# Gathered v rows by four slots of 32 tokens instead of one token's 128 slots, with scaled diagonals as stationary operand

## The chip, the cores and the metric

The kernel runs on one core of a Trainium2 chip. The metric is the device time of one execution in microseconds (us); the figure for the kernel before is the median of three runs. A profile of one further execution is read below. Engines are named as in the profile: PE is the matrix engine (TensorE), PEld its weight loads, DVE the vector engine, ACT the scalar engine, POOL the engine that issues the indirect transfers (GpSimd), SP the one that issues the weight blocks.

## The reference, cut to what matters

Two trunk layers are computed for 128 context tokens and for 256 latent tokens. Each layer has a mixer (four kinds of heads behind one input projection), and then the PEER stage, which is what the change is about:

```python
def peer(x, w_q, sub_keys, u_tab, v_tab):          # 8 heads, 16 of 16384 experts each
    q = (xt @ w_q).reshape(t, 8, 2, 128)
    s = einsum('thpc,hpkc->thpk', q, sub_keys)     # 2 x 128 sub-key scores a head
    s_top, i_top = top_k(s, 16)
    cand     = s_top[..0, :, None] + s_top[..1, None, :]        # 256 candidates
    cand_idx = i_top[..0, :, None] * 128 + i_top[..1, None, :]  # row = key1 * 128 + key2
    best, pos = top_k(cand, 16)
    idx  = take_along_axis(cand_idx, pos)          # (t, 128): 8 heads x 16 slots
    gate = softmax(best)
    act  = gelu(einsum('ted,td->te', u_tab[idx], x))
    return einsum('te,ted->td', gate * act, v_tab[idx])
```

For every token 128 rows of 1024 float32 (4 KB) are fetched from table u and 128 from table v. Row number is key1 x 128 + key2, so two rows with the same second key lie a multiple of 512 KB apart. A token's 16 rows of one head come from a 16 x 16 grid of keys and often share one.

## The kernel before, in words

There are six tiles of 128 tokens, q = 0 to 5: q0 is the context in layer 0, q1 and q2 the latent tokens in layer 0, q3 the context in layer 1, q4 and q5 the latent tokens in layer 1. They form four units: unit 0 is q0, unit 1 is q1 with q2, unit 2 is q3, unit 3 is q4 with q5. Each unit has a mixer; the u and v work of the unit before is interleaved with it by a fixed table (`schedule`, `mix_points`): at given points of its own stream every engine runs the next `item_u` or `item_v` (`gap`). The u and v work of unit 3 has no mixer beside it and makes up the last 720 us.

Gathers. POOL issues one indirect transfer per step s (line 501), 128 rows of 4 KB, one row into each partition of ring slot s % 8. So the ring holds eight transfers, and a slot is refilled only when its reader has raised `rows_used` for it. In a u transfer, partition p holds the row of token p at slot s. In a v transfer before the change, partition p holds slot p of one token, `token(s)` = (s % 4) * 32 + s // 4; its indices are column `token(s)` of `idxT`, which is the transposed table of indices.

v sums. `item_v` on PE works in half steps of four transfers, one for each group of 32 tokens. Each group has its own 32 columns of the PE array and its own 32 partitions of the accumulator `pv`. For each transfer there are two matmuls (512 of the 1024 columns each) with a stationary operand of 128 x 32 from `wcol`. A float32 matmul shows as two records in the profile, so a transfer has four, and all of them together 3072. Before the change the stationary operand is zero but for column m, which holds the token's 128 weights. The zeros are written once (line 1362). ACT writes the eight columns of the next step in one ACTIVATE (`fill_wcol`, line 1310), four buffers deep: the fill for step i+2 waits until PE has used step i-2. PE releases the four slots of a half step during its second matmuls, that is after the fourth transfer has landed.

Start of a tile's v work (`item_gelu` on three engines): ACT runs Gelu on the dot products, DVE multiplies by the gates (line 1844), PE transposes the 128 x 128 result (line 952), ACT copies it to `wT` and fills `wcol` for the steps 0 and 1, and PE's first half step waits for the first fill (line 966). The index table is transposed on PE at the end of a tile's top-k (line 1002) and DVE copies it to `idxT` (line 1808) before it goes on with the gates.

Lines that the prediction speaks of: L501 (POOL, gathers), L524 and L527 (the helpers through which every matmul and every transpose goes), L966 and L971 (PE's waits for the fill and for the rows), L1017 (the helper of every ACTIVATE), L1310 (fill), L1362 (memset), L1808 and L1844 (DVE), L1838 (DVE's dot product of a u transfer).

## Time and profile before

| | |
|---|---|
| median of three runs | 3166.04 us (3154.32 to 3171.97) |
| span of the profiled execution | 3176.3 us |
| PE busy / PEld busy | 63% / 37% |
| DVE busy | 56% |
| POOL busy | 47% (1536 gathers) |
| ACT busy | 12% (814 instructions) |
| gathers' share of the 16 DMA engines | 68.0%, 805.4 MB |
| last 720 us (q4 and q5, u then v) | DMA busy 9 tenths or more in nearly every slice |

The profiled execution has no separate time beside its span; the span is 10.3 us over the median of the runs and 4.3 us over the slowest. In the page, the line of 40 slices gives the busy share of each engine in tenths, 79.4 us a slice. A group's row gives the line, the engine, the operation, what is written and read, the shape and the count, then busy time (overlaps counted once) and the mean duration of one. Where instructions overlap, busy time over count is less than that mean, and it is busy time over count that says how fast they follow each other. A row of the timeline gives the start, the duration and in brackets how long the engine sat idle before, and what ended that.

### The profile page before, as it was taken

The numbers are of one execution on the slowest core, as the hardware profiler recorded it, in microseconds if no ns is written. First come the engines' busy times: TensorE is split into PE (matmuls) and PEld (weight loads), VectorE is DVE, ScalarE is ACT, GpSimd is POOL, SyncE is SP. The second block draws the span as 40 slices with busy tenths as digits, with TensorE's granted clock in tenths as the row PEclk, the third lists the DMA queues.
The fourth block names the chain that finished last, engine by engine and source line by source line (L and its number), as shares of the span: only waits on it lengthen the run. The fifth ranks groups of instructions, "written<-read, shape, count | busy, mean of one in ns | idle before, by whom it ended". The sixth has DMA issues, their size and how long they took to land.

```text
span 3176.3 us, 27801 instructions
## 1 busy us (share of the span) xinstructions
PE 2008.3 (63%) x10194; PEld 1164.2 (37%) x10194; DVE 1763.4 (56%) x3957; ACT 378.2 (12%) x814; POOL 1480.1 (47%) x1540
## 2 busy tenths in 40 slices
PE   5979386668887414438878776677897000067777
PEld 3858275564732413402341165563751000011111
DVE  1622699872286899950070079984176999910000
ACT  1322121112201100000110021112210000000000
POOL 0000144324156565666526634324137777766664
PEclk7979697869998756679989978777999555589999
DMA  6557487547589999999969978656579999999998
GB/s 242 204 197 294 154 338 295 185 150 278 179 288 365 412 385 341 361 379 371 371 229 368 362 279 325 200 171 225 179 252 330 401 410 409 406 364 365 357 352 309
DMA packets 249063, 959.26 MB, mean 302 GB/s; under 512 B 32352, under 2 KB 33504, under 8 KB 231136
## 3 DMA queue, kind: packets, MB, share of 16 engines
q0 software_dynamic: 221184, 805.40, 68.0%
q1 hardware_dynamic: 19584, 142.62, 12.1%
q10 hardware_dynamic: 8160, 9.46, 0.9%
q8 instruction: 82, 1.34, 0.2%
q14 instruction: 53, 0.43, 0.0%
HBM read 955.01 MB, written 2.36 MB: 301 GB/s over the span
## 4 chain that ended last, share of the span: by engine, by line
DVE 26%; DMA 26%; PE 25%; POOL 13%; issue 7%; ACT 2%; ACTq 1%; POOLq 0%; DVEq 0%
PE pb L524 17%; DMA sb_ring<-in_peer_v,sb_idxT 16%; DVE sb_ring L1838 13%; POOL sb_ring L501 13%; DMA sb_ring<-in_peer_u,sb_idxu 8%; PE pv L524 7%; DVE sb_big L1402 1%; PE pb L527 1%; DVE sb_big L1531 1%; DVE sb_big L1550 1%; DVE sb_dec L1492 1%; ACT sb_hT L1017 1%; ACT sb_big L1017 1%; DMA sb_dec<-in_x_prompt 1%; DVE sb_big L1548 1%
## 5 line engine op out<-in xcount | busy, mean ns | idle before, releaser
L501 POOL DMA_INDIRECT sb_ring<-in_peer_u,sb_idxu x768 | 727.9, 948 | 965.4 <-DVE sb_dots L1838 460.9
L501 POOL DMA_INDIRECT sb_ring<-in_peer_v,sb_idxT x768 | 752.0, 979 | 710.0 <-PE pv L524 477.1
L524 PE MATMUL pv<-sb_ring,sb_wcol 128*32 128x512 f32 x3072 | 816.2, 638 | 212.1 <-DMA sb_ring<-in_peer_v,sb_idxT 203.8
L1838 DVE CUSTOM_DVE_ANT_0 sb_ring<-sb_ring,pv 128x1024 f32<-128x1024 f32 x768 | 904.2, 1217 | 27.6 <-DMA sb_ring<-in_peer_u,sb_idxu 14.5
L524 PEld LDWEIGHTS pv<-sb_ring,sb_wcol 128*32 128x32 f32 x3072 | 145.5, 112 | 848.5 <-DMA sb_ring<-in_peer_v,sb_idxT 655.5
L524 PE MATMUL pb<-sb_hT,sb_wring 128*128 128x256 f32 (+1 forms) x1888 | 366.9, 357 | 32.4 <-DMA sb_wring<-in_w_in_blocks 12.7
L524 PEld LDWEIGHTS pb<-sb_hT,sb_wring 128*128 128x128 f32 x1888 | 323.5, 206 | 78.5 <-issue 16.3
L524 PE MATMUL pb<-sb_big 128*128 128x128 f32 (+2 forms) x1888 | 266.5, 315 | 112.9 <-DVE sb_big L1531 82.1
L524 PEld LDWEIGHTS pb<-sb_big 128*128 128x128 f32 (+1 forms) x1888 | 259.7, 225 | 125.1 <-DVE sb_big L1531 87.0
L527 PE MATMUL pb<-sb_cst,sb_dots 128*128 128x128 f32 x6 | 2.7, 451 | 402.1 <-DVE sb_dots L1844 402.1
L1851 DVE COPY sb_accv<-pv 128x1024 f32<-128x1024 f32 x6 | 7.3, 1224 | 392.6 <-PE pv L524 392.5
L524 PE MATMUL pb<-sb_big,sb_cst 128*128 128x256 f32 (+2 forms) x272 | 101.5, 533 | 107.4 <-DVE sb_big L1470 42.2
L1017 ACT ACTIVATE sb_big<-pb 128x512 f32<-128x512 f32 (+3 forms) x184 | 84.9, 467 | 549.8 <-PE pb L524 421.3
L527 PEld LDWEIGHTS pb<-sb_cst,sb_dots 128*128 128x128 f32 x6 | 1.1, 175 | 403.6 <-DVE sb_dots L1844 403.6
L1739 DVE MAX8 sb_xe<-sb_dec 128x8 f32<-128x128 f32 x128 | 28.1, 281 | 171.5 <-ACT sb_cv L1017 94.4
L524 PEld LDWEIGHTS pb<-sb_big,sb_cst 128*128 128x128 f32 x272 | 57.9, 247 | 140.3 <-DVE sb_big L1470 43.9
L1808 DVE CAST sb_idxT<-pb 128x128 uint32<-128x128 f32 x6 | 1.8, 292 | 183.6 <-PE pb L527 183.4
L1732 DVE SCALAR_TENSOR_TENSOR sb_xT<-pb,sb_modT,sb_xT 128x128 f32<-128x128 f32 (+1 forms) x32 | 13.4, 417 | 156.5 <-PE pb L524 156.5
L524 PE MATMUL pb<-sb_wring,sb_hT 128*128 128x256 f32 x336 | 82.8, 408 | 18.6 <-ACT sb_big L1017 14.1
L1017 ACT ACTIVATE sb_wcol<-sb_wT 128x8 f32<-128x8 f32 x96 | 18.3, 212 | 522.4 <-PE pv L524 522.3
L524 PEld LDWEIGHTS pb<-sb_wring,sb_hT 128*128 128x128 f32 x336 | 69.0, 208 | 30.1 <-issue 14.9
L1017 ACT ACT_TABLE_LOAD x57 | 73.1, 1283 | 9.4 <-issue 5.1
(220 smaller groups left out, 1868.0 us busy)
## 6 DMA issues: line engine op xcount, KB each, us to landing
sb_wring<-in_w_in_blocks SPq DMA_DIRECT2D x32, 1024.0 KB, 8.0
sb_ring<-in_w_mod_blocks SPq DMA_DIRECT2D x30, 1024.0 KB, 5.2
sb_wring<-in_w_q_blocks SPq DMA_DIRECT2D x27, 1024.0 KB, 4.9
sb_wring<-in_w_mod_blocks SPq DMA_DIRECT2D x18, 1024.0 KB, 5.0
sb_wring<-in_w_out_blocks SPq DMA_DIRECT2D x13, 1024.0 KB, 7.9
sb_ring<-in_peer_u,sb_idxu POOLq DMA_INDIRECT x768, 7.3
sb_ring<-in_peer_v,sb_idxT POOLq DMA_INDIRECT x768, 6.1
sb_ring<-in_w_in_blocks SPq DMA_DIRECT2D x8, 1024.0 KB, 5.3
```

The costliest lines, as they stand in the source:

```text
L501: pool.indirect_dma_start(ring[:, j, :], None, a["tab_" + kind][l_of(q)], bass.IndirectOffsetOnAxis(ap=of, axis=0)).then_inc(rows_in[j], 16)
L524: return nc.tensor.matmul(out, lhsT, rhs, start=start, stop=stop)
L527: return nc.tensor.transpose(out, in_, ident[0:in_.shape[0], 0:in_.shape[0]])
L1017: return nc.scalar.activation(out, in_, f, **kw)
L1402: last = stt(y, cin[:, k % 2, n:n + NC], convT[:, k, n:n + 1], y, ALU.mult, ALU.add)
L1492: last = stt(dec[:, d, m * 4 + h, :], pb[:, 2 * d + m, h * P:h * P + P], gct[:, i, c:c + 1], con("negm", d, P), ALU.subtract, ALU.add)
L1531: return tt(dst, big_at(512 * d, 4, P), bc1(lvl[:, d, lv, :], 4), ALU.mult)
L1548: tt(x, x, pb[:, 2 + d, :], ALU.add).then_inc(*tick("x_ready", (u, i, d, lv)))
L1550: tt(xt, xt, pb[:, 4 + d, :], ALU.add).then_inc(*tick("xt_ready", (u, i, d, lv)))
L1732: stt(x, pb[:, 4 + j % 2, 0:NC], modT[:, l, 16 + j, g:g + 1], x, ALU.mult, ALU.add) \
L1739: last = dve.max(vals(r)[:, lo:lo + 8], rows(r))
L1838: dve.tensor_tensor_reduce(out=ring[:, j, :], in0=ring[:, j, :], in1=pv[:, :, :].rearrange("p a b -> p (a b)"), scale=1.0, scalar=0.0, op0 ...
```

## The change: what it does, and the diff

A v transfer now takes slots b, 32+b, 64+b and 96+b of the 32 tokens of one group g: partition j*32+a holds the row of token g*32+a at slot j*32+b. For this the tables of indices and of weights are not transposed as a whole but turned in blocks of 32 x 32 (`turn_blocks`): 16 matmuls with 32 columns of the identity as stationary operand, in place of one transpose. Column `turned(s)` = (s % 4) * 32 + s // 4 of the turned tables then serves transfer s. A partition's row now goes to the token of its own lane, so the stationary operand is a diagonal of 32 x 32 in each of the four blocks, scaled by the weight of the partition: ACT makes it from a constant `lane` (128 x 32 of zeros and ones) with the scale read from `wT`, one ACTIVATE for a transfer, eight for a step. As a whole block is written each time, the zeros around the column and their memset go. The number, size and order of gathers, the ring, the matmuls of the v sum and all waits stay as they are.

```diff
-WCOL_WIDTH = STEP * LANES + LANES
+WCOL_WIDTH = STEP * LANES
...
+    parts["lane"] = i[:, None] % LANES == np.arange(LANES)[None, :]
...
-        def token(s):
+        def turned(s):
             return s % GROUPS * LANES + s // GROUPS
...
-                    of = idxu[:, t, s:s + 1] if kind == "u" else idxT[:, t, token(s):token(s) + 1]
+                    of = idxu[:, t, s:s + 1] if kind == "u" else idxT[:, t, turned(s):turned(s) + 1]
...
+            def turn_blocks(bank, src):
+                for gr in range(GROUPS):
+                    for j in range(GROUPS):
+                        last = mm(pb[j * LANES:j * LANES + LANES, bank, gr * LANES:gr * LANES + LANES],
+                                  ident[:, gr * LANES:gr * LANES + LANES], src[:, j * LANES:j * LANES + LANES])
+                return last
...
             def item_gelu(q, t):
                 pe.wait_ge(*done("w_ready", q))
                 take([2], ("wT_copied", q))
-                tr(pb[:, 2, 0:P], dots[:, t, :]).then_inc(*tick("wT_full", q))
+                turn_blocks(2, dots[:, t, :]).then_inc(*tick("wT_full", q))
...
-                                o = j * LANES + LANES - 1 - m
+                                o = j * LANES
                                 last = mm(pv[gr * LANES:gr * LANES + LANES, k, :], wcol[:, i % WCOLS, o:o + LANES],
                                           ring[:, j, k * 512:k * 512 + 512], start=m == 0, stop=m == LANES - 1)
...
-                tr(pb[:, 4, 0:P], posf[:, 0, :]).then_inc(*tick("idxT_full", q))
+                turn_blocks(4, posf[:, 0, :]).then_inc(*tick("idxT_full", q))
...
             def fill_wcol(nv, c):
-                dst = wcol[:, c % WCOLS, LANES - 1:LANES - 1 + STEP * LANES].rearrange("p (m g x) -> p m g x", g=GROUPS, x=LANES)
-                src = wT[:, :].rearrange("p (g m) -> p m g", g=GROUPS)
-                fn(dst[:, :, :, 0], src[:, 2 * c:2 * c + 2, :]).then_inc(wcol_ready, 1)
+                for j in range(STEP):
+                    w = turned(STEP * c + j)
+                    last = fn(wcol[:, c % WCOLS, j * LANES:j * LANES + LANES], con("lane"), ACT.Identity, scale=wT[:, w:w + 1])
+                last.then_inc(wcol_ready, 1)
...
-                dve.memset(wcol[:, :, :], 0.0)
```

ACT's order around the start of tile q0's v work in the mixer of unit 1, before (`sb_dots` is Gelu, `sb_wcol` the fills, the rest is the mixer's; shapes are partitions x elements):

```order
194 L1017 ACTIVATE sb_dots<-sb_dots 128x128
195 L1017 ACTIVATE sb_wT<-pb 128x128
196 L1017 ACTIVATE sb_wcol<-sb_wT 128x8 x3
197 L1017 ACTIVATE sb_big<-pb 128x256 x4
198 L1017 ACTIVATE sb_dec<-pb 128x256 x2
199 L1017 ACTIVATE sb_wcol<-sb_wT 128x8
200 L1017 ACT_TABLE_LOAD
201 L1017 ACTIVATE sb_sm<-sb_sm,sb_epsc 128x2x6
```

The same place of the changed kernel:

```order
194 L1027 ACTIVATE sb_dots<-sb_dots 128x128
195 L1027 ACTIVATE sb_wT<-pb 128x128
196 L1027 ACTIVATE sb_wcol<-sb_cst,sb_wT 128x32 x24
197 L1027 ACTIVATE sb_big<-pb 128x256 x4
198 L1027 ACTIVATE sb_dec<-pb 128x256 x2
199 L1027 ACTIVATE sb_wcol<-sb_cst,sb_wT 128x32 x8
200 L1027 ACT_TABLE_LOAD
201 L1027 ACTIVATE sb_sm<-sb_sm,sb_epsc 128x2x6
```

Nothing changes places; every fill has eight instructions in place of one, and no table load is added (57 in both).

PE's order at the end of unit 3's mixer and in the last 720 us, before (`sb_big` is the index table of q4 and of q5, `sb_dots` the weights, `pv<-sb_ring,sb_wcol` the v sum, one row per instruction of the program, not per record):

```order
443 L524 MATMUL pv<-sb_ring,sb_wcol 32x512 x64
444 L527 MATMUL pb<-sb_cst,sb_big 128x128
445 L524 MATMUL pv<-sb_ring,sb_wcol 32x512 x72
446 L527 MATMUL pb<-sb_cst,sb_big 128x128
447 L524 MATMUL pv<-sb_ring,sb_wcol 32x512 x8
448 L527 MATMUL pb<-sb_cst,sb_accv 128x128 x8
449 L527 MATMUL pb<-sb_cst,sb_dots 128x128
450 L524 MATMUL pv<-sb_ring,sb_wcol 32x512 x256
```

The same place of the changed kernel:

```order
443 L526 MATMUL pv<-sb_ring,sb_wcol 32x512 x64
444 L526 MATMUL pb<-sb_big,sb_cst 32x32 x16
445 L526 MATMUL pv<-sb_ring,sb_wcol 32x512 x72
446 L526 MATMUL pb<-sb_big,sb_cst 32x32 x16
447 L526 MATMUL pv<-sb_ring,sb_wcol 32x512 x8
448 L529 MATMUL pb<-sb_cst,sb_accv 128x128 x8
449 L526 MATMUL pb<-sb_dots,sb_cst 32x32 x16
450 L526 MATMUL pv<-sb_ring,sb_wcol 32x512 x256
```

Here too nothing changes places: twelve transposes in the program (two for each of the six tiles) become 16 small matmuls each.

## Rows read from the trace of the kernel before

**Rows 1.** The page, busy tenths in 40 slices of 79.4 us.
```profile
DVE  1622699872286899950070079984176999910000
DMA  6557487547589999999969978656579999999998
```

**Rows 2.** Busy time in stretches: us, PE, PEld, DVE, ACT, POOL, clock, DMA share, GB/s.
```profile
2680.00:2780.00 100.00, 0.00 (x0) 0.00 (x0) 95.22 (x155) 0.00 (x0) 72.54 (x78) 0.50 1.02 406
2800.00:2960.00 160.00, 126.16 (x448) 21.99 (x440) 0.00 (x0) 2.81 (x13) 104.68 (x112) 1.00 0.98 366
2839.40:2843.40 4.00, 3.52 (x15) 0.79 (x16) 0.00 (x0) 0.00 (x0) 1.77 (x3) 1.00 1.02 412
2845.60:2849.00 3.40, 2.77 (x12) 0.52 (x12) 0.00 (x0) 0.22 (x1) 2.53 (x3) 1.00 0.84 271
2849.60:2855.60 6.00, 5.14 (x18) 0.79 (x16) 0.00 (x0) 0.00 (x0) 3.72 (x4) 1.00 1.04 416
```

**Rows 3.** Chain of waits, 2838 to 2864 us: start, us, what.
```profile
2839.16 6.57 DMA sb_ring<-in_peer_v,sb_idxT
2845.77 1.08 PE pv L524 x6
...
2850.83 6.32 DMA sb_ring<-in_peer_v,sb_idxT
```

**Rows 4.** Groups that touch sb_wcol and other ACT and PE groups, shapes apart.
```profile
L1017 ACT ACTIVATE sb_wcol<-sb_wT 128x8 f32<-128x8 f32 x96 | 18.3, 212 | 522.4 <-PE pv L524 522.3
L1017 ACT ACTIVATE sb_hT<-sb_hT,sb_modT,sb_modA 128x256 f32<-128x256 f32 x32 | 16.2, 587 | 16.4 <-DVE sb_hT L1383 16.4
L1017 ACT ACTIVATE sb_cv<-sb_big,sb_lay 128x128 f32<-128x128 f32 x20 | 8.0, 400 | 93.9 <-DVE sb_big L1402 93.7
L524 PE MATMUL pv<-sb_ring,sb_cpad 128*32 128x256 f32 x480 | 39.0, 451 | 7.1 <-ACT sb_modrow L1017 6.3 <-ACT sb_solW L1017 0.8
L524 PEld LDWEIGHTS pv<-sb_ring,sb_cpad 128*32 128x32 f32 x480 | 14.8, 122 | 17.5 <-issue 10.8 <-ACT sb_solW L1017 1.2
L527 PE MATMUL pb<-sb_cst,sb_dots 128*128 128x128 f32 x6 | 2.7, 451 | 402.1 <-DVE sb_dots L1844 402.1
```

**Rows 5.** Timeline of ACT, a run of one mixer group.
```profile
818.16 4.04 ACT L1017 ACTIVATE sb_hT<-sb_hT,sb_modT,sb_modA 128x256 f32<-128x256 f32 x8 [4.04 <-DVE sb_hT L1383]
```

**Rows 6.** Timeline, start of the v work of q4.
```profile
2792.38 4.59 PE L524 MATMUL pv<-sb_ring,sb_wcol 128*32 128x512 f32 x18 [0.85 <-ACT sb_wcol L1017]
2794.66 0.20 PEld L524 LDWEIGHTS pv<-sb_ring,sb_wcol 128*32 128x32 f32 x7 [1.08 <-DMA sb_ring<-in_peer_v,sb_idxT]
2796.38 0.93 POOL L501 DMA_INDIRECT sb_ring<-in_peer_v,sb_idxT  x1 [3.10 <-PE pv L524]
```

**Rows 7.** Chain of waits, start of the v work of q5.
```profile
2977.96 0.34 PE pb L527
...
2978.63 0.43 ACT sb_wcol L1017 x3
...
2979.10 2.94 PE pv L524 x13
```

**Rows 8.** Timeline, ACT and DVE in the mixer of unit 1.
```profile
724.02 0.21 ACT L1017 ACTIVATE sb_wcol<-sb_wT 128x8 f32<-128x8 f32 x1
725.98 0.30 ACT L1017 ACTIVATE sb_sm<-sb_sm,sb_epsc 128x12 f32<-128x12 f32 x1 [0.44 <-DVE sb_sm L1663]
813.92 0.21 ACT L1017 ACTIVATE sb_wcol<-sb_wT 128x8 f32<-128x8 f32 x1
```

**Rows 9.** Timeline, DVE at the end of unit 3's mixer; then DVE's memsets at the start.
```profile
2451.87 0.29 DVE L1808 CAST sb_idxT<-pb 128x128 uint32<-128x128 f32 x1 [23.73 <-PE pb L527]
...
2.16 1.02 DVE L1362 MEMSET sb_wcol<- 128x1152 f32 x1 [0.19 <-issue]
```

**Rows 10.** Timeline, ACT at the program's start.
```profile
6.24 0.22 ACT L1017 ACTIVATE sb_cpad<-sb_cT 128x16 f32<-128x16 f32 x1 [1.69 <-DMA sb_cT<-in_cT]
```

## The prediction

> **What bounds the kernel now.** I read the line of slices first [rows 1]. In the last nine slices, the 720 us without a mixer, the DMA line is at 8 or 9 tenths throughout. In the first four of them DVE is at 9 (the u work of q4 and q5), in the last four at 0 (the v work, whose sums PE makes). So the gathers bound this part, and the two kinds run unlike: 406 GB/s in a stretch of u, 366 GB/s in a stretch of v [rows 2]. The reader should see that the DMA share is 1.02 in the first and still 0.98 in the second. Whether the v rows are dear to fetch or come too late is the question on which this change turns.
>
> Short stretches of the v part answer it [rows 2]. From 2839.4 to 2843.4 and from 2849.6 to 2855.6 the engines move 412 and 416 GB/s, as fast as in any u stretch. Between them, from 2845.6 to 2849.0, they move 271 GB/s at a share of 0.84. The chain of waits shows why [rows 3]: the last transfer of a half step is issued at 2839.16 and lands 6.57 us later, PE then needs 1.08 us until slots are free, POOL refills four slots, and the last of these goes out at 2850.83, 4.0 us later. From issue to issue that is 11.67 us for eight transfers. At 412 GB/s eight transfers of 0.524 MB would take 10.2 us, and at the stretch's mean of 366 GB/s a round is 11.5 us. The v loop is bound by the round trip through a ring of eight that is released in fours, not by what a row costs. About 1.3 us in each round are dry.
>
> **The gathers after the change.** Count, bytes, slots, waits and the order of release stay. If a fed queue already moves 412 GB/s with the old pattern, another pattern has nothing to speed up there. I take 0 for 768 transfers. Bounds: at best most of the dry time goes, 1.1 us a round, if it is in truth the slow rows that cause it (rival A); at worst the new pattern slows rows. The u transfers, 128 tokens at one slot, mix tokens as the new ones do and reach 406 GB/s, so I put the worst at 0 too.
>
> The pattern itself does change: rows that share their second key lie a multiple of 512 KB apart, and the 16 rows of a head of one token share keys more often than rows of 32 different tokens. The Trainium skill (DMA: Bandwidth & Descriptors, section on latency and other measured facts) has a table on HBM row pitch: copies with a pitch of 512 KiB between partitions reach 207 GB/s, 2 MiB 164, 4 MiB 103, against 214 with a padded pitch. By its first figure the old pattern would lose some 3%, and by the last, for the few pairs that lie 4 MiB apart, more; rival A is what this rule makes of the time. The 412 GB/s of the fed stretches speak against it.
>
> **The fills on ACT.** One ACTIVATE for a step becomes eight with 32 elements and a scale from memory. Nearest rows: 12 elements with one operand column take 0.30 us [rows 8], 128 elements with one 400 ns [rows 4], so 32 take about 320. Neighbours overlap: 32 ACTIVATEs with two operand columns are busy 16.2 us, 506 ns each, where one lasts 587 ns [rows 4], and three old fills take 0.43 us together at 0.21 each, 0.11 us apart [rows 7]. With 80 to 100 ns of overlap I take them 0.22 us apart: 0.32 + 7 x 0.22 = 1.85 us for a fill against 0.21, that is 1.6 us more. Bounds: without any overlap 8 x 0.32 = 2.6, so 2.4 more; at the old spacing 8 x 0.11 = 0.9, so 0.7 more. Over 96 fills ACT gets 155 us of work more. It is 12% busy, so this counts only where somebody waits:
> - Steady v work: the fill of step i+2 is made when step i-2 is used, two rounds of 11 us ahead. Cost 0; the 522 us that ACT waits for PE before fills [rows 4] hide it.
> - In the mixers ACT makes the fill in its own order and whatever follows waits. After the fill at 813.92 the next ACTIVATE starts at 818.16, 4 us later [rows 5, 8], and so it is for most of the 64 fills there: more than 1.6 us of slack. The exception is 724.02, which a table load and the tiny `sb_sm` follow; that one waited 0.44 us only for DVE [rows 8], and DVE waits for it. There are three such places (one each in units 1, 2 and 3, the one in unit 2 with two fills together): 1.2 + 3.2 + 1.2 = 5.6 us at most. I take 2, since behind them PE has v steps to do.
> - At the start of each tile's v work PE waits for the first fill: 1.6 us more each.
>
> **The turned blocks on PE.** A transpose of 128 x 128 lasts 0.45 us [rows 4]. In its place come 16 matmuls, 32 records. The trace has no matmul with 32 x 32 outputs. The nearest has a 32-column stationary operand, in the four column groups in turn, with 256 columns: 480 records in 39.0 us busy, 81 ns each, and their weight loads 14.8 us, 31 ns each [rows 4]. With 32 columns I take the weight load as the pace: 32 x 31 ns = 1.0 us, so 0.5 more. Bounds: 0 more if they overlap better still; with the mean duration of such a load, 122 ns, and no overlap at all, 32 x 122 ns = 3.9 us, 3.4 more. There are twelve: six before the weights' copy, six for the indices.
>
> **Starts of v work.** Added to each: 1.6 + 0.5 = 2.1 us. At q5 the chain of waits runs straight through transpose, copy, fill, PE [rows 7], with the ring full, and q0, q1, q2, q3 look alike: 5 x 2.1 = 10.5 us. At q4 it is otherwise: PE starts at 2792.38 but stands until 2794.66 for the fourth transfer [rows 6], 2.3 us of slack that cover the 2.1. Cost there 0. POOL, queued behind PE's release (it had waited 3.10 us, [rows 6]), is who would pay.
>
> **Index tables.** DVE waits for PE's turned table before it goes on to the gates, at the end of unit 3's mixer with 23.73 us of waiting behind PE's own v steps [rows 9]. The 0.5 us are added to PE just there. Six times 0.5 is 3 us; half of them have other work beside: 1.5 us.
>
> **The memset.** 1.02 us of DVE at 2.16 us [rows 9] goes. ACT, which waits for it, then still waits for a load until 6.24 us [rows 10], which hides it: 0. `sb_cst` grows by 32 columns in 3090: 0.
>
> **Sum.** 10.5 + 2 + 1.5 = 14 us on the profiled execution's 3176.3 us, so 3190. That execution is 10.3 us over the median of the runs; on the median 3166.0 the same 14 us give 3180.
>
> **Rivals.**
> A. The old rows were slow, and the change ends it. For it: v moves 366 GB/s against 406, and the dry time might be engines that fall behind on a few slow rows, since a transfer counts as landed only when its slowest engine is done. Against it: full speed in the fed stretches. Price: 1.1 us a round, from 11.5 at 366 GB/s to 10.3 at the 406 of u, in the stretches where the gathers set the pace: the 64 rounds of q1, q2, q4, q5 and some 9 each at the ends of q0 and q3, 82 in all, so 90 us. With the 14 added: 3166 + 14 - 90 = 3090. If half of it comes true, 3135. The nine at each end are an estimate: some 105 us of full DMA before q0's and q3's v work ends.
> B. The additions sit at their upper bounds: fills 2.4 us more, blocks 3.4 us more. Starts 5 x 5.8 = 29, and q4 3.5 beyond its slack; index tables 6 x 3.4 = 20, half 10; mixer 2.0 + 4.8 + 2.0, say 8. About 51 us: 3217. For it: PE is at its lower clock, 0.50 or 1.2 GHz, when the u work ends [rows 2], so small matmuls are slow just at a start. Against it: the four column groups visibly overlap [rows 4]. It decides from a fill of 2.2 us more and blocks of 1 us more, where the sum passes 16 us.
> C. ACT's mixer work is delayed as a whole: in q0's and q3's v work, where the mixer sets the pace, each of 32 fills costs its 1.6 us: 51 us more, 3231. For it: ACT is in the chain between PE and DVE in attention. Against it: the slack after most fills [rows 8].
> D. Nothing to be seen: the starts are made up for, since after a pause the queue is empty and transfers land sooner; 3168.
>
> **Chances.** The forecast (3170 to 3190) 0.45, D 0.12, A whole or half 0.17, B 0.21, C 0.05. A measurement of this kernel tells a change from none at about 0.5%, 16 us: below 3150 is faster, above 3182 slower. Of the forecast's 0.45, 0.15 lies above 3182, so faster 0.17, same 0.43, slower 0.40. The forecast's own range is 3168 to 3192. For 8 in 10 I go down to the half of A, 3130, and up to most of B, 3208.
>
> **What would show it.** In the profile after: fills x768 with a mean near 320 ns and some 175 us busy, no more; the stretch 2800 to 2960 at 360 to 370 GB/s and rounds of 11.3 to 11.6 us; starts of q5 2 us later from transpose to first v matmul. The forecast is wrong if the v stretch moves 390 GB/s or more (A), if 16 small matmuls take over 2 us (B), or if the mixers of units 1 and 3 grow by more than 10 us each (C).

## The result, and the profile after

| | before | after |
|---|---|---|
| median of nine runs each | 3169.02 us | 3182.59 us |
| ratio, 95% interval | 1 | 1.0038 [1.0022, 1.0053] |
| span of the profiled execution | 3176.3 us | 3179.6 us |
| ACT | 12%, 814 instructions | 17%, 1486 instructions |

The change makes the kernel 0.38% slower, 13.6 us. Forecast were 14 us, added to the 3166.04 us of the first three runs: 3180 us, against 3182.59. The spans of the two profiled executions differ by only 3.3 us. The first gather is issued at 361.9 us in the one and at 353.2 in the other, and in the runs below that beginning lies anywhere from 352 to 365, so single spans are not compared to less than 10 us here. From the first gather to the end it is 2814.4 us before and 2826.4 after.

The profile of the changed kernel, its groups for the scaled diagonals and the turned blocks, shapes apart (busy us, mean ns of one, idle time ahead and what ended it):

```profile
L1027 ACT ACTIVATE sb_wcol<-sb_cst,sb_wT 128x32 f32<-128x32 f32 x768 | 170.6, 308 | 437.7 <-PE pv L526 437.5
L526 PE MATMUL pb<-sb_dots,sb_cst 128*32 128x32 f32 x192 | 3.9, 244 | 402.4 <-DVE sb_dots L1854 402.4
```

One scaled diagonal takes 308 ns, and 768 keep ACT busy for 170.6 us, 222 ns each, where 320 and 175 were forecast. The 96 old fills took 18.3 us [rows 4]. ACT's wait for PE ahead of the fills is still 437.7 us, of 522.4 before, and the whole kernel is only 13.6 us longer: nearly all of the 152 us came out of ACT's idle time. Six turns, 192 records, are busy for 3.9 us, 0.65 us each; the six transposes took 2.7 [rows 4].

The stretches of the last 460 us, after, with the columns of [rows 2]:

```profile
2680.00:2780.00 100.00, 0.00 (x0) 0.00 (x0) 95.13 (x155) 0.00 (x0) 72.40 (x78) 0.50 1.03 409
2800.00:2960.00 160.00, 125.69 (x446) 21.76 (x442) 0.00 (x0) 22.23 (x99) 104.34 (x112) 1.00 0.97 359
3000.00:3160.00 160.00, 126.52 (x457) 22.59 (x450) 0.00 (x0) 19.84 (x88) 104.69 (x112) 0.99 0.98 368
```

The u stretch moves 409 GB/s (406 before) and the v stretches 359 and 368, where before had 366 and 360. ACT works eight times as long in them, and POOL issues 112 gathers in 160 us as before. The round is the same too. The chain of waits after, one round, to be set beside [rows 3]:

```profile
2843.35 6.57 DMA sb_ring<-in_peer_v,sb_idxT
...
2849.96 1.08 PE pv L526 x6
...
2855.02 6.37 DMA sb_ring<-in_peer_v,sb_idxT
```

6.57 us of transfer, 1.08 us of PE, 4 us until the fourth slot is refilled: 11.67 us, to the hundredth the round of before. The loop is bound by the ring's round trip in both kernels.

What the change costs shows where a tile's v work starts. The start of q3's, before and then after (timeline: start, us, and in brackets the idle time ahead):

```profile
2163.91 0.48 PE L527 MATMUL pb<-sb_cst,sb_dots 128*128 128x128 f32 x1 [10.24 <-DVE sb_dots L1844]
2164.42 0.28 ACT L1017 ACTIVATE sb_wT<-pb 128x128 f32<-128x128 f32 x1 [4.14 <-PE pb L527]
2164.73 0.43 ACT L1017 ACTIVATE sb_wcol<-sb_wT 128x8 f32<-128x8 f32 x3
2165.20 1.08 PE L524 MATMUL pv<-sb_ring,sb_wcol 128*32 128x512 f32 x4 [0.82 <-ACT sb_wcol L1017]
```

```profile
2169.33 0.66 PE L526 MATMUL pb<-sb_dots,sb_cst 128*32 128x32 f32 x32 [10.24 <-DVE sb_dots L1854]
2170.05 0.28 ACT L1027 ACTIVATE sb_wT<-pb 128x128 f32<-128x128 f32 x1 [4.36 <-PE pb L526]
2170.36 2.44 ACT L1027 ACTIVATE sb_wcol<-sb_cst,sb_wT 128x32 f32<-128x32 f32 x11
2172.42 1.08 PE L526 MATMUL pv<-sb_ring,sb_wcol 128*32 128x512 f32 x4 [2.44 <-ACT sb_wcol L1027]
```

From the first record of the transpose or turn to ACT's copy it is 0.51 us before and 0.72 after; from the copy to the first matmul of the v sum 0.78 and 2.37. Together 1.29 and 3.09, so 1.80 us more. The other starts are alike (1.80 to 1.98 more): over all six, 7.64 us before and 18.63 after, 11.0 us more. For q5's, which the prediction named, the chain of waits after reads:

```profile
2982.78 0.70 PE pb L526 x32
...
2983.51 0.29 ACT sb_wT L1027
...
2983.82 1.81 ACT sb_wcol L1027 x8
...
2985.91 3.23 PE pv L526 x13
```

That is 3.13 us from turn to first matmul, against 1.14 (2977.96 to 2979.10, [rows 7]): 2.0 more, where 2.1 were forecast.

### The profile page after: what moved, and what is told of

Same layout as the page of the kernel before. It is cut to its first block, busy times and chain, and to the rows that moved or that the text cites. A ratio compares the mean times of both kernels' runs of the same rounds, so it can differ in the third digit from the quotient of the medians.

```text
span 3179.6 us, 29216 instructions
## 1 busy us (share of the span) xinstructions
PE 1996.4 (63%) x10566; PEld 1157.8 (36%) x10566; DVE 1762.5 (55%) x3956; ACT 529.7 (17%) x1486; POOL 1476.6 (46%) x1540
## 4 chain that ended last, share of the span: by engine, by line
DVE 26%; PE 25%; DMA 25%; POOL 13%; issue 7%; ACT 3%; ACTq 0%; POOLq 0%; DVEq 0%
PE pb L526 17%; DMA sb_ring<-in_peer_v,sb_idxT 16%; DVE sb_ring L1848 13%; POOL sb_ring L503 13%; PE pv L526 7%; DMA sb_ring<-in_peer_u,sb_idxu 7%; DVE sb_big L1412 1%; DVE sb_big L1541 1%; PE pb L529 1%; DVE sb_big L1560 1%; DMA sb_wring<-in_w_q_blocks 1%; ACT sb_hT L1027 1%; ACT sb_big L1027 1%; DMA sb_dec<-in_x_prompt 1%; DVE sb_dec L1502 1%
## 5 line engine op out<-in xcount | busy, mean ns | idle before, releaser
L1027 ACT ACTIVATE sb_wcol<-sb_cst,sb_wT 128x32 f32<-128x32 f32 x768 | 170.6, 308 | 437.7 <-PE pv L526 437.5
L526 PE MATMUL pb<-sb_big,sb_cst 128*32 128x32 f32 (+3 forms) x464 | 106.3, 399 | 131.1 <-DVE sb_big L1480 42.0
L526 PEld LDWEIGHTS pb<-sb_big,sb_cst 128*128 128x128 f32 (+1 forms) x464 | 62.3, 194 | 167.2 <-DVE sb_big L1480 43.7
```

What stands on the lines that cost most here:

```text
L526: return nc.tensor.matmul(out, lhsT, rhs, start=start, stop=stop)
L1027: return nc.scalar.activation(out, in_, f, **kw)
```

## The experiments

Twelve runs follow, on three chips: the first four together with before on one, the next four on a second, the last four on a third. Each ratio is to the kernel before on the same chip. In all where only one part of the change is made, and in the one that masks the row numbers, the sum over v weights rows other than those of the reference, or adds them to other tokens; the number and size of all transfers stay.

**The gather pattern alone.** The kernel before, with the index table turned in blocks and all else left:

```diff
-                tr(pb[:, 4, 0:P], posf[:, 0, :]).then_inc(*tick("idxT_full", q))
+                turn_blocks(4, posf[:, 0, :]).then_inc(*tick("idxT_full", q))
```

> The kernel before with one part of the change: the index table is turned in blocks, so the v gathers fetch four slots of 32 tokens; fills and the weights' transpose stay as before (weights and rows then don't belong together, the sum is not the reference's). Theory (the pattern of rows costs nothing either way, the round trip through the ring paces the v work): +0 to +3 us against before, ratio 1.000 to 1.001, a v stretch at 355 to 370 GB/s. Rival A (rows of one token are slow to fetch): 45 to 90 us faster, ratio 0.97 to 0.985, 380 GB/s or more. Rival A' (the new pattern is a little slower to fetch and makes the 13.6 us of the change): +8 us or more.

Measured: 1.0024 [1.0010, 1.0038]. Rival A's 3% is not there, nor any gain. The theory's 1.001 is at the lower edge of the interval: 7.6 us of cost where it had 3 at most. By its size that is what A' expected, a new pattern that is a little slower to fetch. The trace doesn't bear A' out where gathers set the pace: from the first v gather of q4 to the end it is 393.5 us, 392.7 in the kernel before. Where the 7.6 us are lost stays open.

**The fills alone.** The kernel before, with eight scaled diagonals for a step and without the memset:

```diff
-                fn(dst[:, :, :, 0], src[:, 2 * c:2 * c + 2, :]).then_inc(wcol_ready, 1)
+                for j in range(STEP):
+                    w = token(STEP * c + j)
+                    last = fn(wcol[:, c % WCOLS, j * LANES:j * LANES + LANES], con("lane"), ACT.Identity, scale=wT[:, w:w + 1])
+                last.then_inc(wcol_ready, 1)
...
-                dve.memset(wcol[:, :, :], 0.0)
```

> The kernel before with the other part: eight scaled diagonals on ACT for a step in place of one strided copy, no memset; gathers and transposes as before (the stationary operand is then not the one that the rows need). Theory: the fills make most of the change, 5 to 6 starts at 1.6 us each and 2 us in the mixers, +8 to +12 us, ratio 1.0025 to 1.004; from the weights' copy to the first v matmul 1.6 us more. Rival (the pattern or the turned blocks make it): +0 to +3 us, ratio 1.000 to 1.001. Rival C (fills delay the mixers as a whole): +15 us or more.

Measured: 1.0053 [1.0032, 1.0074], 16.8 us. The theory had 12 us at most, and its 1.004 is inside the interval; the middle of it lies where rival C began, at 15 us. So the fills by themselves cost time, and more than was expected. Its timeline has 2.37 us from copy to first matmul at five starts and 2.40 at the sixth, as in the changed kernel: 9.6 us by the starts.

**Both tables turned, old fills.**

```diff
-                tr(pb[:, 2, 0:P], dots[:, t, :]).then_inc(*tick("wT_full", q))
+                turn_blocks(2, dots[:, t, :]).then_inc(*tick("wT_full", q))
...
-                tr(pb[:, 4, 0:P], posf[:, 0, :]).then_inc(*tick("idxT_full", q))
+                turn_blocks(4, posf[:, 0, :]).then_inc(*tick("idxT_full", q))
```

> Both tables turned in blocks, so the new gather pattern and all twelve turns, with the old single fill (not the operand that the rows need). Theory: twelve turns at some 0.3 us each, half of them on the path: +1 to +4 us, ratio 1.000 to 1.0015, that is the change without its fills. Rival B (turns are the dear part): +8 us or more. Rival A: 45 us faster or more.

Measured: 1.0026 [1.0009, 1.0043], 8.3 us, against 1.0024 with one table. The theory had 4 us at most, rival B 8 or more. B's reason isn't there, since a turn takes PE 0.65 us and not 3.9; the second turn, 0.2 us at six starts, can't be told from nothing.

**Every row a multiple of 512 KB from every other.** This is the sharpest test of rival A and of the rule behind it. The v row numbers keep only their first key:

```diff
-                dve.tensor_copy(idxT[:, t, :], pb[:, 4, 0:P]).then_inc(*tick("idxT_copied", q))
+                dve.tensor_copy(idxT[:, t, :], pb[:, 4, 0:P]).then_inc(*step())
+                dve.wait_ge(*stepped())
+                ts(idxT[:, t, :], idxT[:, t, :], 16256, None, ALU.bitwise_and).then_inc(*tick("idxT_copied", q))
```

> The kernel before, but every row number of the v gathers is cut down to a multiple of 128, so all rows of a transfer lie a multiple of 512 KB apart and more of them are equal (wrong rows, same count and bytes; one small DVE operation more for each tile). It puts what rival A fears in every transfer. Theory (a fed queue takes rows as they come, the pattern is nothing to this ring): within 0.5% of before, v stretch 350 to 370 GB/s. Rival A (rows at this pitch collide): v stretches fall well below 340 GB/s and the time rises by 50 us or more.

Measured: 1.0005 [0.9989, 1.0021]. With all 128 rows of each v transfer at that pitch the stretch from 2800 to 2960 moves 362 GB/s against 366:

```profile
2800.00:2960.00 160.00, 128.40 (x444) 22.10 (x445) 0.00 (x0) 2.59 (x12) 102.74 (x111) 0.99 0.98 362
```

Rival A has fallen. The pitch table of the Trainium skill (DMA: Bandwidth & Descriptors, section on latency and other measured facts) was measured on direct copies; the trace here does not agree for gathers of 4 KB rows by one core. Two limits of the test: with only the first key left more rows of a transfer are the same row than before, and it speaks of the pitch of 512 KB and its multiples in a ring that waits for its round trip.

**The fills doubled.** The changed kernel, each diagonal in two halves of 16 columns, 16 ACTIVATEs for a step:

```diff
-                    last = fn(wcol[:, c % WCOLS, j * LANES:j * LANES + LANES], con("lane"), ACT.Identity, scale=wT[:, w:w + 1])
+                    for half in range(2):
+                        o = j * LANES + 16 * half
+                        last = fn(wcol[:, c % WCOLS, o:o + 16], con("lane")[:, 16 * half:16 * half + 16], ACT.Identity, scale=wT[:, w:w + 1])
```

> The changed kernel with each diagonal written in two halves, 16 ACTIVATEs for a step in place of eight (same values). A fill then takes some 3.4 us in place of 1.8. Theory (what the fills cost is their latency at the six starts and little in the mixers): 1.6 us more at each start and as much again in the mixers as the first eight cost, +8 to +16 us against the changed kernel, so +20 to +30 us against before, ratio 1.006 to 1.0095. Rival C (ACT as a whole holds up the mixers): each of 64 fills costs its time, +60 us or more against the changed kernel. Rival (fills are hidden, the change's time is in the pattern and the turns): no more than +3 us against the changed kernel, ratio 1.003 to 1.005.

Measured: 1.0100 [1.0076, 1.0124]. Its group and its start of q3's v work:

```profile
L1027 ACT ACTIVATE sb_wcol<-sb_cst,sb_wT 128x16 f32<-128x16 f32 x1536 | 312.1, 294 | 357.2 <-PE pv L526 357.0
```

```profile
2186.18 0.65 PE L526 MATMUL pb<-sb_dots,sb_cst 128*32 128x32 f32 x32 [10.25 <-DVE sb_dots L1856]
...
2190.75 1.08 PE L526 MATMUL pv<-sb_ring,sb_wcol 128*32 128x512 f32 x4 [3.91 <-ACT sb_wcol L1027]
```

The halves follow each other every 0.20 us. From turn to first matmul it is now 4.57 us in place of 3.09, 1.48 more, 8.6 over six starts. Against the changed kernel's 1.0038 the ratio is 0.62% higher, some 20 us, where 8 to 16 were expected; the two ratios come from different chips and are each good to about 0.2%. So the fills seem to cost beside the starts too, 11 us here and 7 in the run of the fills alone, but far from rival C: 51 us more than the changed kernel, one more fill's delay for each of 32 steps, would put it at 1.02.

**Slots released singly: is the round trip the bound?** The kernel before, with the two loops of a half step exchanged. Both matmuls of a transfer follow each other, and its slot is released at once. Nothing is left out of the computation.

```diff
-                        for k in range(2):
-                            for gr in range(GROUPS):
+                        for g0 in range(0, GROUPS, 1):
+                            for k, gr in [(k, gr) for k in range(2) for gr in range(g0, g0 + 1)]:
```

> The kernel before with the two loops of the v sum exchanged: for each transfer both matmuls at once, so each slot is released by itself and not in fours. Nothing else. Theory (the v loop is paced by the round trip of a ring that is released in fours): rounds of eight transfers fall from 11.4 towards 10.2 us, some 80 rounds, 60 to 95 us faster, ratio 0.970 to 0.981, if the four column groups still overlap; v stretch 390 GB/s or more. Rival 1 (slow rows or the DMA engines pace it): no change within 0.5%. Rival 2 (in this order PE blocks behind one column group, four records at 0.43 us each are 1.7 us a transfer, over the 1.28 that a transfer needs): rounds of 13 us or more, 100 us slower.

Measured: 0.9714 [0.9688, 0.9739], 3088.7 us, 89 us under before on that chip. The old rows, the old fill, and 410 GB/s in a stretch of pure v work:

```profile
2750.00:2850.00 100.00, 100.00 (x310) 27.61 (x309) 0.00 (x0) 1.96 (x9) 74.04 (x80) 1.00 1.03 410
```

80 gathers in 100 us where the four-slot release gave 70. POOL now issues one after the other with the 0.30 us that it needs between two in any case:

```profile
2801.87 0.94 POOL L501 DMA_INDIRECT sb_ring<-in_peer_v,sb_idxT  x1 [0.30 <-issue]
2803.11 0.94 POOL L501 DMA_INDIRECT sb_ring<-in_peer_v,sb_idxT  x1 [0.30 <-issue]
...
2805.59 0.93 POOL L501 DMA_INDIRECT sb_ring<-in_peer_v,sb_idxT  x1 [0.30 <-PE pv L524]
```

Of the dry time of the prediction, 1.3 us in each of 82 rounds or 107 us, 89 us were to be had, and none by other rows. POOL is now near its own pace too: at 0.94 and 0.30 us it can issue 80.6 gathers in 100 us. And PE has no idle time left in that stretch (100.00 us busy). Its weight loads show how it goes, one row for each record or, with x2, for two (timeline):

```profile
2800.79 0.14 PEld L524 LDWEIGHTS pv<-sb_ring,sb_wcol 128*32 128x32 f32 x2 [0.28 <-DMA sb_ring<-in_peer_v,sb_idxT]
2801.25 0.11 PEld L524 LDWEIGHTS pv<-sb_ring,sb_wcol 128*32 128x32 f32 x1 [0.32 <-issue]
2801.68 0.11 PEld L524 LDWEIGHTS pv<-sb_ring,sb_wcol 128*32 128x32 f32 x1 [0.32 <-issue]
2802.07 0.14 PEld L524 LDWEIGHTS pv<-sb_ring,sb_wcol 128*32 128x32 f32 x2 [0.28 <-DMA sb_ring<-in_peer_v,sb_idxT]
```

The records of one transfer start 0.43 us apart, and the first of the next transfer, in another column group, goes together with the last of this one. So a transfer takes PE 1.28 us, as long as its gather takes at 410 GB/s. Rival 2 had 1.7.

**The same in pairs.** Two transfers at a time:

```diff
-                        for k in range(2):
-                            for gr in range(GROUPS):
+                        for g0 in range(0, GROUPS, 2):
+                            for k, gr in [(k, gr) for k in range(2) for gr in range(g0, g0 + 2)]:
```

> The kernel before with the v sum in pairs of transfers, slots released in twos. Theory of the round trip: part of the gain of releasing by ones, 40 to 95 us faster. If PE blocks behind a column group in the order by ones, two groups in turn need 0.86 us a transfer, below 1.28, and this order gains where that one loses.

Measured: 0.9724 [0.9697, 0.9752]. Pairs are enough to keep the queue fed. From 2750 to 2850 us this run moves 410 GB/s too, with 78 gathers and PE busy for 91.13 us, so neither PE nor POOL sets that rate.

**The changed kernel, released singly.** The same exchange of loops, in the changed kernel:

> The changed kernel with slots released one by one. Theory: the cost of the change stays (starts and mixers, +8 to +20 us against the same order with the old fill) and the gain of the release is the same, so 0.975 to 0.988 of before. Rival A in a new form (the new pattern helps once the ring no longer hides it): it is as fast as the old pattern in this order or faster.

Measured: 0.9783 [0.9760, 0.9806], 3109.03 us, 20 us above the old pattern with the same release. Here the change costs 0.7%. The six starts are 10.8 us longer (7.75 us in the one, 18.59 in the other). The v work of q0 and of q3, from its first gather to the first of the next tile, is 4.0 and 6.6 us longer, of which 3.6 are their starts. But 4.7 of q3's 6.6 us are a matter of PE's clock: one block of mixer work takes 5.4 us at a granted 1.00 in the one and 10.1 at 0.50 in the other, as shown further down for the first pair of traces.

**The turn four times over.** The kernel before, with the index table turned four times ahead of the old transpose, which overwrites it:

```diff
+                for _ in range(4):
+                    turn_blocks(4, posf[:, 0, :])
                 tr(pb[:, 4, 0:P], posf[:, 0, :]).then_inc(*tick("idxT_full", q))
```

> The kernel before, with the index table of each tile turned in blocks four times ahead of the old transpose, which then overwrites it: the gather pattern, the fills and the weights are those of before, and PE has 4 x 0.65 us more ahead of the index table of each of the six tiles. Theory (the pattern of rows costs nothing; a turn on PE counts where DVE waits for it, about half of the six): 5 to 10 us slower, ratio 1.0015 to 1.003; if every one of the 15.6 us is on the path, 1.005. Rival (turning is free, and what the run with only the index table turned cost, 1.0024, is the new pattern of rows): 0.9995 to 1.0005.

Measured: 1.0064 [1.0039, 1.0088]. The four turns take 1.9 us, less than the 2.6 expected, since they overlap:

```profile
356.52 1.93 PE L524 MATMUL pb<-sb_big,sb_cst 128*32 128x32 f32 x128 [26.43 <-DVE sb_big L1810]
...
358.90 0.29 DVE L1818 CAST sb_idxT<-pb 128x128 uint32<-128x128 f32 x1 [1.97 <-PE pb L527]
```

Six times 1.9 is 11 us, 0.35%, and the interval begins at 0.39%: even in full the turns don't reach what was measured. So PE's work ahead of the index tables seems to count in full and not by half, with something on top that the run doesn't show; 3.2 us of it may be the gap told at the end of the next part. For one turn in place of a transpose, 0.2 us, that is 1.2 us at six tiles. It doesn't explain the 7.6 us of the gather pattern alone.

**Each diagonal released by itself.** The changed kernel, PE waiting per transfer and not per step:

```diff
-                        if h == 0:
-                            pe.wait_ge(wcol_ready, nv * STEPS + i + 1)
...
+                                    pe.wait_ge(wcol_ready, STEP * (nv * STEPS + i) + j + 1)
...
-                    last = fn(wcol[:, c % WCOLS, j * LANES:j * LANES + LANES], con("lane"), ACT.Identity, scale=wT[:, w:w + 1])
-                last.then_inc(wcol_ready, 1)
+                    fn(wcol[:, c % WCOLS, j * LANES:j * LANES + LANES], con("lane"), ACT.Identity, scale=wT[:, w:w + 1]).then_inc(wcol_ready, 1)
```

> The changed kernel, but each of the eight ACTIVATEs of a fill releases its own transfer, and PE waits for one diagonal ahead of each first matmul instead of for all eight ahead of a step. Theory (the fill of 1.6 us counts at the starts of v work, where PE waits for the first one): the first matmul comes 1.5 us sooner at five or six starts, 7 to 9 us less than the changed kernel, so a ratio to the kernel before of 1.001 to 1.002, and at the start of q5 about 1.7 us from the last turning matmul to the first matmul of the v sum in place of 3.1. Rival (the fills count in the mixers, where ACT's later work is delayed): nothing is won, 1.0035 to 1.0045, though the start of q5 is shorter.

Measured: 1.0068 [1.0042, 1.0094]; the changed kernel beside it 1.0079 (below). The timeline does what was expected at all six starts, 0.89 us from copy to first matmul in place of 2.37. Here q3's:

```profile
2188.23 0.65 PE L526 MATMUL pb<-sb_dots,sb_cst 128*32 128x32 f32 x32 [10.24 <-DVE sb_dots L1852]
2188.95 0.28 ACT L1026 ACTIVATE sb_wT<-pb 128x128 f32<-128x128 f32 x1 [4.35 <-PE pb L526]
2189.26 2.02 ACT L1026 ACTIVATE sb_wcol<-sb_cst,sb_wT 128x32 f32<-128x32 f32 x9
...
2189.84 2.13 PE L526 MATMUL pv<-sb_ring,sb_wcol 128*32 128x512 f32 x7 [0.95 <-ACT sb_wcol L1026]
```

That is 8.9 us over six starts. The medians differ by 6.6 us, but by the intervals that is not told from nothing. As a time it is inconclusive, and far above the 1.001 to 1.002 expected.

**Both releases at once.** The changed kernel with slots and diagonals both released singly:

> The changed kernel with ring slots released one by one (both matmuls of a transfer together) and the fills released one by one as well. Released one by one, the old pattern ran at 0.9714 of the kernel before and the new one at 0.9783. Theory (the difference of 20 us lies to about 8 us in the fills at the starts, the rest in the turns and the mixers): 0.975 to 0.9765, that is 6 to 9 us less than with whole fills. Rival (it is ACT's longer work inside the mixers): 0.978 to 0.979.

Measured: 1.0098 [1.0068, 1.0127]. Both theories missed by 3%. The gain of single release, 2% on the second chip, is not there on the third. The kernel before with its slots released singly did not run on the third.

**The changed kernel again,** beside these:

> The changed kernel once more, beside the others of this call. Theory: 1.003 to 1.005 of the kernel before (first measured 1.0038). Rival (the first figure was the spread of runs): under 1.002.

Measured: 1.0079 [1.0054, 1.0105], slower than before again, and by more than the first time.

What differs is the third chip. The kernel before takes 3220.22 us there, and 3178 on the second. A stretch of u work in layer 1, from 2620 to 2740, in the changed kernel released singly on the second chip, and in the changed kernel on the third:

```profile
2620.00:2740.00 120.00, 0.00 (x0) 0.00 (x0) 113.39 (x185) 0.00 (x0) 86.84 (x94) 0.50 1.03 409
```

```profile
2620.00:2740.00 120.00, 0.00 (x0) 0.00 (x0) 105.46 (x172) 0.31 (x1) 80.33 (x86) 0.50 0.98 373
```

And v work of layer 0, from 1700 to 1760, in the changed kernel released singly on the second chip, and with both releases on the third:

```profile
1700.00:1760.00 60.00, 60.00 (x190) 16.79 (x188) 0.00 (x0) 10.61 (x42) 42.86 (x47) 1.00 1.03 409
```

```profile
1700.00:1760.00 60.00, 57.85 (x169) 14.88 (x168) 0.00 (x0) 9.02 (x40) 39.44 (x43) 1.00 0.98 367
```

A fed queue gives 409 on the second chip and 367 to 373 on the third. Yet the u tables of layer 0 are read at 412 there too (from 1080 to 1140, changed kernel):

```profile
1080.00:1140.00 60.00, 29.50 (x139) 26.20 (x139) 56.82 (x105) 6.84 (x15) 35.65 (x39) 0.76 1.02 412
```

That is not a matter of the table alone. From 1340 to 1380, in the u work of the next tile from the same table, it is 388 GB/s there and 410 on the second chip, and in layer 1 q4's u work runs at 387 (2520 to 2580) and q5's at 373. So on the third chip the same gathers are slow in some stretches and not in others. At 370 GB/s eight transfers take 11.3 us, and the ring's round trip of 11.67 leaves some 0.3 us to win where 1.4 were, 25 us over 82 rounds. That would explain the larger part of what is missing, but not all: of those 25 us nothing shows in the ratio. The six runs spread over 28 us, and the profiled one, at the low end with 3237, is 15 us under the profiled run of the changed kernel beside it. Why the gathers are slow there, no run shows.

## Why the prediction was right, step by step

**The bound: right.** The v loop was said to be bound by the round trip through a ring released in fours. The exchange of loops, same rows and same bytes, raised 366 GB/s to 410 and took 89 us away.

**The gathers at 0: right.** The v stretches after move 359 and 368 GB/s, the round is 11.67 us in both, and the run with all rows 512 KB apart reads 1.0005. The rule on pitch, weighed against the fed stretches' 412 GB/s [rows 2], does not act here.

**A fill at 1.6 us more: right.** Measured 1.56 to 1.62 at the six starts. The working was right too: 308 ns for 320, 214 ns apart for 220. The Trainium skill (ScalarE: Activation LUTs, section on what ACT_TABLE_LOAD costs) gives 280 ns + 0.833 ns an element with one pointer operand, and 93 ns of overlap: by an estimate from these, 307 ns, and 214 apart. The trace agrees with both.

**A turn at 0.5 us more: too high.** It is 0.2. The step took 31 ns for each of 32 weight loads, a pace read from loads of another group; the 32 records take 0.65 us, 20 ns each. At q5 it is 0.36, since the old transpose took only 0.34 us there [rows 7].

**q4's start at 0: this step failed.** The prediction put 2.3 us of slack there, PE standing from 2792.38 to 2794.66 for the fourth transfer. After:

```profile
2792.41 0.65 PE L526 MATMUL pb<-sb_dots,sb_cst 128*32 128x32 f32 x32 [331.04 <-DVE sb_dots L1854]
...
2795.56 7.43 PE L526 MATMUL pv<-sb_ring,sb_wcol 128*32 128x512 f32 x32 [2.49 <-ACT sb_wcol L1027]
...
2799.43 0.94 POOL L503 DMA_INDIRECT sb_ring<-in_peer_v,sb_idxT  x1 [4.80 <-PE pv L526]
```

PE starts 3.15 us after the turn begins, and the first refill goes out 7.02 us after it, where before it was 5.32 (2791.06 to 2796.38): 1.7 us were paid. The refill follows PE's first v matmul by 3.87 us here and by 4.00 before [rows 6]; at three of the other five starts of before, where the ring has long been full, it follows by 3.87 too, at two by 3.45 and 3.20. So nearly all of those 4 us were PE's own time from a standing start, not the transfer's. Real slack was some 4.00 - 3.87 = 0.13 us; by the same count two further traces with the old fill, the gather pattern alone (4.33) and the masked row numbers (4.24), have 0.46 and 0.37; four others, at 3.56 to 3.87, have none. The row of 1.08 us "<-DMA" was read as a wait that sets the end, without asking how long PE takes at a start that nobody delays.

**The starts: 11.0 us measured for 10.5.** Two errors cancelled: 1.8 us in place of 2.1, at six starts in place of five. And this is the delay of the first matmul, which the prediction took for the cost. Whether a tile ends later by as much is another question, and the traces answer it only in part. From the end of DVE's product with the gates to the end of the last v matmul, q5 takes 185.3 us before and 184.8 after; three further traces with the old fill (the gather pattern alone, both tables turned, the masked row numbers) have 183.7 to 185.3, the fills alone 183.3. So at q5, with slots released in fours, the 2 us don't show at the end. With slots released singly they do: 167.2 and 169.0. At q1 and q2 the same count grows by 6.2 and 5.8 us, over three times what their starts add. So the 10.5 us of the sum were delays and not shown to be costs, and that the total fits is in part luck.

**Mixers at 2 us and index tables at 1.5: too low, by how much is open.** The fills alone cost 16.8 us [10, 24], of which the starts are 9.6; the doubled fills and the two kernels released singly leave 7 to 11 us beside the starts. The index table alone cost 7.6 us [3, 12] where six turns of 0.2 us should cost 1.2. The bound of 5.6 us for the mixers counted the places where the next ACTIVATE follows a fill closely, and took "more than 1.6 us of slack" behind the others from one row.

Between the two profiled executions the v work of q0 is 5.7 us longer and that of q3 3.9 shorter. For q3 the traces show a reason other than the fills' own time, TensorE's granted clock. Ahead of the 33rd v gather of q3 the mixer gives PE the same work in both. Chain of waits, before and then after, and a window over each (PEclk is the number before the DMA share):

```profile
2201.56 1.51 PE pb L527 x6
2203.07 5.01 PE pb L524 x24
2208.09 3.57 PE pv L524 x13
2201.50:2211.50 10.00, 9.94 (x46) 6.96 (x46) 0.42 (x1) 1.38 (x4) 0.34 (x1) 0.50 0.49 192
```

```profile
2208.75 0.90 PE pb L529 x6
2209.65 2.63 PE pb L526 x24
2212.27 1.85 PE pv L526 x13
2208.70:2214.20 5.50, 5.45 (x48) 3.91 (x50) 0.42 (x1) 2.84 (x11) 0.94 (x1) 1.00 0.90 337
```

The same records take 10.1 us at the lower clock (0.50) and 5.4 at the higher (1.00), and the gather waits for them. In the fourteen traces this place of q3 stands at 0.50 in eleven and at 1.00 in three, that of q0 seven and seven, with old and new fills on either side. So one pair of traces can't size what the change costs in a mixer, and whether the fills shift the clock on average stays open. A third place was overlooked: the v work of q1 and q2, in unit 2's mixer, is 8.3 and 3.9 us longer, with 1.8 us of start in each, where the prediction gave that mixer 3.2 us at most. By the fills alone they are 5.4 and 5.9 us longer, and by both turned tables with the old fills 7.3 and 3.2, so this isn't the fills alone either.

**What doesn't add up.** The starts give 11.0 us and the mixers some 7 more, yet the whole was 13.6 on the first comparison. The parts alone (0.53% and 0.26%) sum to 0.79%, more than the whole on the first comparison (0.38%, up to 0.53) and just what the third chip shows for it. On the second chip, released singly, the change cost 0.7%, on the third 0.79%. So the forecast of 14 us matched one measurement closely; over three comparisons the cost is 14 to 25 us, and the upper end contains something that the prediction did not have. Part of it on the third chip can be seen, though not explained. At q4's start ACT's copy comes 6.6 us after the turn's end:

```profile
2851.17 0.66 PE L526 MATMUL pb<-sb_dots,sb_cst 128*32 128x32 f32 x32 [356.53 <-issue]
...
2858.42 0.28 ACT L1027 ACTIVATE sb_wT<-pb 128x128 f32<-128x128 f32 x1 [184.45 <-remote]
```

Such gaps, between one engine's end and the start of the next, add some 9.5 us over the six starts of that run, 9.5 and 9.0 in the two with diagonals released singly, and 3.2 in the run with four turns beside them; in all traces of the other chips they are under 0.2 us. "remote" means that the profile shows nobody who released ACT. The kernel before has no trace on that chip, so whether it has such gaps is open.

**The rivals.** A is refuted. B's upper bounds were not met (fill 1.6 and not 2.4, turn 0.2 and not 3.4). C as worked out, 51 us, is refuted, but its mechanism, fills that delay ACT's other work, seems to be there at a fifth of its size, if that rest is not the clock's. D's total, 3168, is not what was measured, and q4 pays at its start, but at q5 of the two profiled executions what D described is seen.

## What to carry to other kernels

Before changing what a transfer reads, look for a short stretch in which its queue is fed and read the rate there: if that is as high as anywhere, the loop around the transfer is the bound, and how soon a slot is released decides. Here exchanging two loops took 2.9%, on a chip where the fed rate was 409 GB/s; it is the fastest version of all that ran (3088.7 us), and it rests on one chip. Where the fed rate is 370 the changed kernel with both releases won nothing; the kernel before was not tried there. And before calling a wait slack, compare with the same place elsewhere in the trace where nobody waits: what PE needs there anyway is not slack. Look at the granted clock of both places as well before a few microseconds between two traces are put down to a change.

## What the runs showed of the hardware that was not expected

- Matmuls of one column group in a row overlap those of the next group only at the seam. In the order by ones the records of a transfer start 0.43 us apart though each lasts 0.59, and only its last goes together with the next transfer's first: 1.28 us for four records. In pairs the same work keeps PE busy for 91 of 100 us at the same 410 GB/s.
- The rate of a fed gather depends on the chip and the stretch: 409 to 412 GB/s for u and v on the second chip, and on a third 412 in one stretch, 387 and 388 in others and 367 to 373 in more, with 412 and 388 from one and the same table. A gain that fills dry time has to be measured on more than one chip.
- Back to back, ACTIVATEs of 128 x 16 with a scale operand follow each other every 0.20 us, of 128 x 32 every 0.21: half the columns saved 0.01 us.
- An execution's beginning, before the first gather, varies by 13 us between kernels that are nearly alike up to there (352 to 365), as much as the whole change. It goes with PE: in the first 350 us PE is busy for 252.9 us at a granted clock of 0.85 where the first gather comes at 352.0 (fills alone), and for 268.95 us at 0.81 where it comes at 364.6 (the changed kernel again).
